# A hybrid decode step: sample states updated for two heads in one product, with block-structured masked keys

## What is computed

```python
def chunked_scalar_decay(q, k, v, logd, S0):
    ...
        G = jnp.cumsum(lc, axis=-1)
        A = jnp.einsum('bhid,bhjd->bhij', qc, kc) * _pair_decay(G, incl)
        o = (jnp.einsum('bhij,bhjv->bhiv', A, vc)
             + jnp.einsum('bhid,bhdv->bhiv', qc * jnp.exp(G)[..., None], S))
        S = (S * jnp.exp(G[..., -1])[..., None, None]
             + jnp.einsum('bhjd,bhjv->bhdv', kc * jnp.exp(G[..., -1:] - G)[..., None], vc))
```

## Time and profile before

| | us |
|---|---|
| median of 3 runs | 2556.91 (2554.68 to 2557.4) |
| the profiled execution | 2557.54 |
| its span | 2555.6 |
| busy: PE | 2378.2 (93%) |
| busy: DVE | 1628.2 (64%) |
| busy: ACT | 1094.3 (43%) |
| busy: POOL | 183.0 (7%) |

### The profile page before, as it was taken

The page is one execution under the profiler, slowest core; times in us unless marked ns, Lnnn a source line. Parts: engine busy times, 40 slices in busy tenths (PEclk is TensorE's granted clock), DMA queues, the critical chain, the costliest instruction groups (busy, mean ns, idle before and its releaser), DMA issues.

```text
span 2555.6 us, 36507 instructions
## 1 busy us (share of the span) xinstructions
PE 2378.2 (93%) x14562; PEld 2060.8 (81%) x14562; DVE 1628.2 (64%) x1902; ACT 1094.3 (43%) x1300; POOL 183.0 (7%) x249
## 2 busy tenths in 40 slices
PE   7899989989999988999899998899999999999986
PEld 6888979866999977798888767777877878778765
DVE  4444673455655464454852745689898898988965
ACT  3331432122444243233321231466666666666643
POOL 0110201112000000211110110000000000000000
PEclk8988999688999999889897888799999999999988
DMA  5323432022455442333321302789998899988942
GB/s 183 115 86 114 144 110 68 33 104 85 143 165 168 132 152 86 105 116 124 118 94 40 113 33 82 262 316 344 330 335 321 312 346 329 330 322 316 347 153 82
DMA packets 163735, 457.40 MB, mean 179 GB/s; under 512 B 9864, under 2 KB 10410, under 8 KB 161010
## 3 DMA queue, kind: packets, MB, share of 16 engines
q1 hardware_dynamic: 159938, 432.13, 47.8%
q0 software_dynamic: 3632, 22.95, 2.5%
HBM read 444.04 MB, written 11.00 MB: 178 GB/s over the span
## 4 chain that ended last, share of the span: by engine, by line
PE 39%; DVE 8%; issue 3%; ACT 1%; DMA 0%; DVEq 0%; SPq 0%; POOL 0%; ACTq 0%; POOLq 0%
PE ps L1303 4%; PE ps L1305 4%; PE ps L1304 4%; DVE weights_low L2340 4%; PE ps L1322 3%; PE ps L1323 3%; PE ps L1324 3%; PE ps L764 2%; PE ps L797 2%; PE ps L765 2%; PE ps L766 2%; PE ps L1288 1%; PE ps L913 1%; PE ps L1271 1%; PE ps L1103 1%
## 5 line engine op out<-in xcount | busy, mean ns | idle before, releaser
L2340 DVE TENSOR_TENSOR weights_low<-expert_raw,weights_high 128x2048 fp32r<-128x2048 f32 x264 | 603.9, 2290 | 74.3 <-PE ps L1324 49.4
L1672 ACT ACTIVATE weights_high<-expert_raw 128x2048 fp32r<-128x2048 f32 x264 | 506.7, 1919 | 259.4 <-PE ps L1305 165.1
L764 PE MATMUL ps<-u_high,mix_high 128*128 128x288 f32 x1800 | 564.4, 314 | 6.6 <-DVE mix_low L1792 4.9
L765 PE MATMUL ps<-u_low,mix_high 128*128 128x288 f32 x1800 | 549.8, 305 | 0.0
L766 PE MATMUL ps<-u_high,mix_low 128*128 128x288 f32 x1800 | 546.8, 304 | 0.0
L1792 DVE TENSOR_TENSOR mix_low<-ring,mix_high 128x1024 fp32r<-128x1024 f32 x254 | 316.2, 1249 | 283.4 <-ACT mix_high L1413 271.9
L764 PEld LDWEIGHTS ps<-u_high,mix_high 128*128 128x128 f32 x1800 | 356.9, 198 | 19.6 <-issue 12.3
L765 PEld LDWEIGHTS ps<-u_low,mix_high 128*128 128x128 f32 x1800 | 357.2, 198 | 0.9
L766 PEld LDWEIGHTS ps<-u_high,mix_low 128*128 128x128 f32 x1800 | 356.9, 198 | 0.0
L1413 ACT ACTIVATE mix_high<-ring 128x1024 fp32r<-128x1024 f32 x254 | 266.9, 1053 | 165.2 <-DMA ring<-in_stream 64.3
L1303 PE MATMUL ps<-weights_high,gathered_high 128*128 128x512 f32 x704 | 279.2, 397 | 3.3 <-DVE gathered_low L2352 3.3
(11 more groups left out here) (389 smaller groups left out, 3153.4 us busy)
## 6 DMA issues: line engine op xcount, KB each, us to landing
expert_raw<-in_stream SPq DMA_DIRECT2D x264, 1024.0 KB, 6.1
ring<-in_stream SPq DMA_DIRECT2D x290, 512.0 KB, 3.3
mixer_memory<-in_state POOLq DMA_DIRECT2D x8, 1024.0 KB, 5.7
state_s<-mixer_memory POOLq DMA_DIRECT2D x8, 1024.0 KB, 4.9
mixer_memory<-in_const POOLq DMA_DIRECT2D x2, 1240.0 KB, 5.9
h<-in_x SPq DMA_DIRECT2D x1, 1152.0 KB, 5.3
y<-arena POOLq DMA_DIRECT2D x1, 1152.0 KB, 4.4
state_p<-mixer_memory POOLq DMA_DIRECT2D x8, 128.0 KB, 4.9
```

The lines of the kernel that those rows point to most:

```text
L764: mm(out, high[k], u_high[:, k, :], start=k == 0, stop=False)
L765: mm(out, high[k], u_low[:, k, :], start=False, stop=False)
L1672: A(w_high[:, n % HIGHS], raw[n % RAWS], ACT.Copy).then_inc(w_high_ready, 1)
L2340: tt(w_low[:, n % LOWS], raw[n % RAWS], w_high[:, n % HIGHS].bitcast(F32), ALU.subtract).then_inc(w_low_ready, 1)
```

## The change

Two heads whose state rows are the two halves of the 128 partitions share a product. Their token rows are stacked: the first head on partitions 0 to 31, the second on 32 to 63. The masked keys are block-structured: 64 rows and, for each sequence, 128 columns, the first 64 of which hold the first head's keys in its own 32 rows and zeros below, the other 64 the second head's keys in the lower 32 rows and zeros above (`seq_half`). In SSD it is the keys in `kdec` that are block-structured (a memset, then two products on DVE), and the masked values that are stacked. So the rows of the samples have to stand on partitions 32 to 63 as well. `transposes`, `prep` and the end of GDN's solve make them a second time with products that write there, and DVE and ACT work on 64 rows instead of 32 in the preparation (`pads_twice`). POOL makes masks for a pair of heads, 64x1024 (in SSD 64x512). The first pair's goes to `masks`, the second's, except in SSD, to the memory of `pt` (the scores), so that it waits for `o_ps` and no longer for PE's use of the first; the decay of the state comes behind it.

```diff
+PBASE, NPAIR = [0, 2, 4, 6], 10
...
+    c["seq_half"] = pad(((row % SAMP // DSEQ == col // 2) & (row // SAMP == col % 2)) * 1.0)
...
+        def mask_of(n, pair):
+
+            if n == SSD:
+                return masks[0:64, 512 * (pair % 2):512 * (pair % 2) + 512]
+            return masks[0:64, :] if pair == 0 else pt.rearrange("p h c -> p (h c)")[0:64, 0:1024]
+
+        def pads_twice():
+
+            return [(P, slice(0, 2)), (2 * SAMP, slice(2, 3))]
...
+                for k in range(KD):
+                    last = mm(bank(M + 1)[32:64, 32:48], u[:, k, SEQ:TOK], wsm[:, k, 16:32], start=k == 0, stop=k == KD - 1)
                 last.then_inc(small_ps, 1)
...
+                last = mm(bank(M + 3)[32:64, 0:256], glrt[0:17, SEQ:TOK], wgk[0:17, :], start=True, stop=True)
                 last.then_inc(gk_ps, 1)
...
-                mm(r[0:32, 32:48], C("after_s")[0:32], ls[0:32, 2, :], start=True, stop=True)
+                for f in range(2):
+                    mm(r[32 * f:32 * f + 32, 32:48], C("after_s")[0:32], ls[0:32, 2, :], start=True, stop=True)
...
-                mm(bank(M + 2)[0:32, 0:256], C("after_s")[0:32], gx[0:32, 2, :], start=True, stop=True)
+                for f in range(2):
+                    mm(bank(M + 2)[32 * f:32 * f + 32, 0:256], C("after_s")[0:32], gx[0:32, 2, :], start=True, stop=True)
...
                         tr(bank(M + b)[0:nt, 128 * c:128 * c + 128], src, C("ident"))
+                        if b == 2 and (c >= 2 if n == SSD else c % 2 and n != GDN):
+                            mm(bank(M + b)[32:64, 128 * c:128 * c + 128], src, C("ident"), start=True, stop=True)
...
+                        if b == 2:
+                            last = mm(bank(M + 4)[32:64, 128 * c:128 * c + 128], ksrc[:, t0:t0 + nt], C("ident"), start=True, stop=True)
                 last.then_inc(vk_ps, 1)
...
+                def with_samples(pair):
+
+                    pe.wait_ge(masked_ready, L * NPAIR + PBASE[n] + pair + 1)
+                    mk = mask_of(n, pair)
+                    if n == SSD:
+                        last = mm(bank(M + pair), kdec[0:64, 2, 128 * pair:128 * pair + 128], mk, start=True, stop=True)
+                    else:
+                        for b in range(NSEQ):
+                            last = mm(bank(M + 2 * pair + b // 4)[:, dv * (b % 4):dv * (b % 4) + dv],
+                                      mk[:, 128 * b:128 * b + 128], vtok[0:64, 2, 256 * pair:256 * pair + 128],
+                                      start=True, stop=True)
+                    last.then_inc(masked_used, 1)
...
                     mm(o, kdec[:, 0, kc], v[:, 0], start=True, stop=False)
                     mm(o, kdec[:, 1, kc], v[:, 1], start=False, stop=True)
-                    pe.wait_ge(masked_ready, gh + 1)
-                    mk = masks[0:32, 512 * (hh % 2):512 * (hh % 2) + 512]
-                    if n == SSD:
-                        last = mm(bank(M + pair)[r, :], kdec[0:32, 2, kc], mk, start=True, stop=True)
-                    else:
-                        for b in range(NSEQ):
-                            last = mm(bank(M + 2 * pair + b // 4)[r, dv * (b % 4):dv * (b % 4) + dv],
-                                      mk[:, 64 * b:64 * b + 64], v[0:32, 2], start=True, stop=True)
-                    last.then_inc(masked_used, 1)
+                    if hh % 2 if n != SSD else hh >= 4:
+                        with_samples(hh // 2 if n != SSD else hh - 4)
...
+                for hh in (1, 3):
+                    last = mm(bank(M + 5)[32:64, 128 * hh - 128:128 * hh], xt_s[0:32, hh, :],
+                              vtok[0:32, 2, 128 * hh:128 * hh + 128], start=True, stop=True)
                 last.then_inc(vn1_ps, 1)
...
+                if n in (GLA, RET):
+                    cp(vtok[odd, 2, :].rearrange("p (q f v) -> p q f v", q=2, f=2)[:, :, 0, :],
+                       bank(M + 2)[odd, :].rearrange("p (q f v) -> p q f v", q=2, f=2)[:, :, 1, :])
+                elif n == SSD:
+                    tt(vtok[odd, 2, 0:256].rearrange("p (h v) -> p h v", h=4), bank(M + 2)[odd, 256:512].rearrange("p (h v) -> p h v", h=4),
+                       xs[odd, 2, 12:16].unsqueeze(2).to_broadcast([32, 4, 64]), ALU.mult)
+                    V.memset(kdec[0:64, 2, :], 0.0).then_inc(dve_step, 1)
+                    dve.wait_ge(dve_step, steps.next())
+                    for f in range(2):
+                        rf = slice(32 * f, 32 * f + 32)
+                        tt(kdec[rf, 2, :].rearrange("p (q f d) -> p q f d", q=4, f=2)[:, :, f, :],
+                           bank(M + 4)[rf, 64 * f:64 * f + 64].unsqueeze(1).to_broadcast([32, 4, 64]),
+                           kde[rf, 2, 8 + 4 * f:12 + 4 * f].unsqueeze(2).to_broadcast([32, 4, 64]), ALU.mult)
...
-                cp(vtok[0:32, 2, :], bank(M + 5)[0:32, :]).then_inc(vn1_ready, 1)
+                cp(vtok[0:32, 2, :], bank(M + 5)[0:32, :])
+                cp(vtok[32:64, 2, :].rearrange("p (q f v) -> p q f v", q=2, f=2)[:, :, 0, :],
+                   bank(M + 5)[32:64, :].rearrange("p (q f v) -> p q f v", q=2, f=2)[:, :, 0, :]).then_inc(vn1_ready, 1)
```

89 lines of the change are left out of this document (51 added, 38 removed).

## The result

The changed kernel took 2521.15 us (median of 4 runs, 2520.12 to 2525.2), the kernel before 2555.8 (4 runs, 2554.43 to 2557.4): a ratio of 0.9859, 95% interval 0.9843 to 0.9874, so 1.4% faster. The forecast was 2522 us, in a range of 2511 to 2541. In a later comparison the changed kernel took 2523.06 us beside 2556.88, ratio 0.986 (0.9842 to 0.9878). The profiled execution took 2520.12 us, its span is 2517.9.

A forecast was written before the change was run, and what follows sets the result against it. PE fills the state stretches, but DVE decides whether shortening them shortens the kernel. Gains of 16.3 + 4.0 + 17.1 + 3.8 + 10.4 = 51.6 us, less 15.9 added, take 2557.5 to 2522 us, range 2511 to 2541.

The forecast's parts named there:

- The bound: Eight state stretches: PE fills them, but DVE, which adds products to the state, decides whether shorter ones shorten the kernel.
- GLA: GLA's state stretches: 14.26 and 14.21 us become 6.1 each, 16.3 us saved, as DVE waits for PE there.
- the tile behind: Weight tile after GLA's stretch: 5.19 us at clock 0.59 becomes 3.1 at full clock, 2.0 a layer, 4.0 in all.
- SSD: SSD's state stretches: 14.84 and 16.29 us become 7.0 each, 17.1 saved, plus 3.8 in the branch products behind.
- RET and GDN: PE's savings there become waits for DVE; DVE gains 2.6 us in each per layer, 10.4 in all.
- the gap of 1.09: RET: DVE's 1.09 us gap before a low half, waiting for ACT, disappears; part of RET's 2.6 us gain.
- only what DVE gains itself counts: RET and GDN: PE saves 4 and 8 us a layer, but that turns into waits; only DVE's 10.4 us count.
- Added work: Copied sample rows, preparation and DVE copies on PE's or DVE's path: 7.95 us a layer, 15.9 added; bounds 8 to 20.
- Moved masks: POOL builds pair masks ahead of PE, decay after: 0 on the path, 0.4 in GLA if cover is short.
- The clock falling as before: New stretches and work behind them: clock falls after as long as before, gain 38.0 instead of 51.6, 2535 us; 30%.
- The wider weights: GLA and SSD: each of 80 sample records takes 0.06 us more, 4.8 us return, 2527 us; 9%.
- DVE binding behind GLA and SSD: Behind GLA and SSD: DVE binds too, only its own 10.4 us come through, 15.9 are added, 2563 us; 4%.

The follow-up runs named there:

- pairs_gla_ssd: Changed kernel, but only GLA and SSD share products; RET and GDN keep their old masks and 64 sample products each: 2533.53 us, ratio 0.9895.
- busy_wait: Changed kernel plus 18 unused products a layer on PE during its wait behind GDN for DVE's first branch sum: 2515.59 us, ratio 0.9835.
- added_only: Changed kernel with all doubled rows kept, but masks, sample products and decay as in the kernel before, nothing shared: 2573.52 us, ratio 1.0066.
- samples_four: Changed kernel with each shared sample product issued four times, same result: 2575.69 us, ratio 1.0069.
- early_sums: Changed kernel with two of GDN's branch sums moved earlier on DVE, between the convolution pairs: 2517.03 us, ratio 0.9841.

## Why the prediction was right, point by point

**The bound.** PE was to be followed and DVE to decide: right. GLA and SSD gave their time, RET and GDN gave together about what DVE was to gain (pairs_gla_ssd: 10.5 to 12.4 us, forecast 10.4).

**The sum.** The gain in span was 37.7 us, the forecast's 35.7 (51.6 less 15.9). By intervals the terms of the forecast come to -3.7 to the first state of GLA, 18.2 from GLA to RET, 2.3 from RET to GDN, 1.7 from GDN to SSD and 17.2 behind SSD, over both layers. The table has 0.2, 18.2, 7.9, -4.4 and 15.8. So two terms were off by some 6 us, one by 4, and they cancel: that the time came within 1 us is luck, that the gain lay behind GLA and SSD is not.

**GLA.** Forecast 8.15 for the stretch and 2.0 for the tile behind, less RET's added transposes (1.04): 9.1 a layer. Measured 9.10 and 9.13. Inside, the stretch was worth more (14.26 to 5.14), since the prompt products overlap, and RET's added work cost 0.2; PE then waited 0.42 us for a low half in the tile behind and more further on (its waits for low halves went from 4.9 to 13.9 us in all). The equality of the sum is of terms that were each off by 1 to 2 us.

**SSD.** Forecast 17.1 for both stretches, measured 18.2 (14.84 and 16.29 to 6.47 each). The overlap of the prompt products is the term that I missed. With the branch products behind the stretch, for which the forecast had 3.8 more, the lead over the kernel before grew from 11.9 to 22.8 us in the first layer and from 27.2 to 39.8 in the second: 23.4 for a forecast of 20.9.

**RET and GDN.** The sum held, the terms did not. RET gave more: 4.0 a layer to the next state, with GDN's own added work inside, where I had 2.6 less 1.4 (four products of 0.26 and a copy of 0.4). The masks beside DVE cost it 2.2 us, more than the 1.5 of the earlier trace rows; the gap of 1.09 went too, as forecast; the rest is not told apart from the clock. GDN gave less: to the next state the kernel lost 1.4 and 3.0 us, with SSD's added work inside. Against the kernel that has this work alone (111.63 and 111.62 us) it lost 0.4 in both layers, where I had 2.6 of gain. The step that failed is "only what DVE gains itself counts": DVE was 15.1 us ahead at GDN's state copy (505.96 before, 490.89 after) and 13.2 at SSD's first look at its values (538.07 and 524.85). I had written that PE's gain goes over to a wait, but left out that a longer wait costs a second time, in the clock behind it (0.58 for 0.71). busy_wait shows that price, 1.7 us a layer.

**Added work.** 15.9 forecast, 16.2 measured (added_only). In after's first layer GLA seemed free (186.69 us at its first state product, 186.84 before). That belonged to this execution: the same kernel came to that point at 189.53 us in its second measurement, and samples_four, with the same list up to there, at 191.98. The clock between 150 and 160 us was 0.83 in the first and 0.66 in the other two. What decides it is open.

**Moved masks.** "0 on the path" was too small a claim. They stood ready as forecast (POOL's timeline of after: the second mask, then the decay)

```profile
175.14 1.90 POOL L2593 TENSOR_TENSOR mixer_memory<-arena,const 64x1024 f32<-64x1024 f32 x1 [19.72 <-PE ps L966]
177.00 4.84 POOL L2575 TENSOR_TENSOR mixer_memory<-mixer_memory 128x1024 f32<-128x1024 f32 x2
```

and gave DVE 2.2 us a layer in RET, and the kernel 1.7 to 3.8.

**The rivals.** The clock falling as before (30%): out, 1.00 in all eight; and samples_four shows that the fall came with the form of the products, not with the length by which I had weighed it. My argument against this rival (RET held for 9.2 us, longer than the new 6 to 7) led to the right side for the wrong reason. The wider weights: a record went from 0.1175 to 0.124, not by 0.06. The Trainium skill (TensorE: Matmul & The Clock Gate, LDWEIGHTS (loading the stationary operand)) would have the load longer by 53 ns. The load records agree (132 ns at the median for 32x64, 188 for 64x128), but from start to start of the products only 6 ns of it show. DVE binding behind GLA and SSD: DVE had no idle time before GLA's state copy (0.42 us of PE's waiting instead), SSD's still waited 4 us. Unchanged parts: measured by equal instructions of DVE, after's lead went from 22.8 to 21.3 us over the dense block and what follows it, and from 39.8 to 37.7 over the experts. That is open, and it cancels part of what the overlap gave.

## What to carry to other kernels

Before fusing two small products into a block-structured one, write them alternately, if their outputs lie on different halves of the partitions: here that gave all of the time that the fusion gave, with the second head's rows on partitions of their own. Read the granted clock of the stretches behind a change as well as of the changed one, since both the form of small products and a new idle time of PE are paid there. A gain that "goes over to a wait" is not neutral: here 11.2 us of waiting cost 1.7 us on top, which useless work in its place brought back.

## What was not expected of the hardware

- Two products of 64 weight columns each, on different column halves and neighbours in PE's list, ran in the time of one: 0.059 us a record against 0.1175, whether they read the same 32 rows or others. With 16 of one head before 16 of the other it was 0.102. In SSD the two took 1.01 us against 2.0. The Trainium skill (TensorEngine Tiling (Array Packing), Tiling Modes, Key Properties) says that different tiles of the array can load and multiply in parallel; the traces agree, and add that the order of the list decides whether they do.
- The granted clock fell from 2.4 to 1.2 GHz while PE was full with products of 32 rows and 64 columns (0.67 over GLA's 14.26 us), and not in 15.86 us of products of 64 rows and 128 columns. Alternating ones on rows 0 to 31 alone kept 1.00 within their 4.97 us and had 0.83 behind them; on rows 0 to 63, in a kernel with other work ahead, 1.00 behind them too. With one edit between two kernels, the second heads' products on rows 0 to 31 as well instead of 32 to 63, GDN's stretches had 0.70 and 0.64 instead of 0.87.
- After PE's idle time of 11.2 us the clock was 0.58 in the next five us, after 5.3 us 0.71, and in early_sums 16 records after an idle time of 2.29 us took 5.81 us instead of 4.2. Work that nobody needs, in its place, was the faster choice.
